# Two attention mixers and two hybrid blocks on one core: where a few small transposes stand between the projection products

## The reference, cut to what matters

```python
xbc = jax.nn.silu(causal_depthwise_conv(xbc, conv_w, conv_b))
xs, bm, cm = jnp.split(xbc, [SSM_INNER, SSM_INNER + SSM_GROUPS * D_STATE], axis=-1)
y = ssd_chunked(xs, dt, a_neg, bm, cm) + d_skip[:, None] * xs
y = rmsnorm_2(y * jax.nn.silu(z), ssm_norm)   # in two groups of 512
return jnp.concatenate([attn, y], axis=-1) @ w_out
```

## Time and profile before

| | |
|---|---|
| runs, median (lowest to highest) | 850.31 us (849.8 to 850.94) |
| the profiled execution: its time, and its span from first to last instruction | 850.76 us, 848.4 us |
| busy: PE, DVE, ACT, POOL | 841.2, 623.7, 535.3, 201.4 us |
| the chain that ended last, by engine | PE 94%, ACT 4%, DVE 1%, issue 1% |
| TensorE clock granted | 0.999 over the span |
| DMA | 146.19 MB, mean 172 GB/s |

### The profile page before, as it was taken

One profiled execution on the slowest core, in us unless ns is written; L12 is line 12 of the kernel. 1 busy time (PEld: TensorE's weight loads), 2 busy tenths in 40 slices (PEclk: granted clock), 3 DMA queues, 4 the chain that ended last, 5 costly groups with the idle time before them and its releaser, 6 DMA issues.

```text
span 848.4 us, 12997 instructions
## 1 busy us (share of the span) xinstructions
PE 841.2 (99%) x4631; PEld 706.4 (83%) x4631; DVE 623.7 (74%) x1109; ACT 535.3 (63%) x1035; POOL 201.4 (24%) x175
## 2 busy tenths in 40 slices
PE   9999999999999999999999999999999999999997
PEld 6887888888888888888888888888888888888885
DVE  6867865778776797688888546576797688888544
ACT  7677466866897864655556434787874655665533
POOL 0221053110152420033333000152330043334000
PEclk9999999999999999999999999999999999999999
DMA  9823563445534436665665555444347566565631
GB/s 319 297 72 132 165 205 128 150 149 182 172 125 148 140 133 200 205 201 182 186 196 190 207 199 176 151 149 149 103 147 224 176 200 196 186 180 184 228 116 49
DMA packets 94307, 146.19 MB, mean 172 GB/s; under 512 B 5925, under 2 KB 54565, under 8 KB 94245
## 3 DMA queue, kind: packets, MB, share of 16 engines
q1 hardware_dynamic: 92212, 139.58, 50.5%
q0 software_dynamic: 1296, 4.72, 1.6%
q10 hardware_dynamic: 736, 1.07, 0.4%
HBM read 144.32 MB, written 1.05 MB: 171 GB/s over the span
## 4 chain that ended last, share of the span: by engine, by line
PE 94%; ACT 4%; DVE 1%; issue 1%; POOL 0%; ACTq 0%; DVEq 0%
PE bank L1396 54%; PE bank L1349 17%; PE bank L1352 9%; PE bank L1273 6%; PE bank L1577 1%; PE bank L1481 1%; PE bank L1457 1%; ACT hi L1596 1%; PE bank L1454 1%; ACT hyb_prob L1812 1%; PE bank L1484 1%; PE bank L1278 0%; PE bank L1294 0%; PE bank L1292 0%; PE bank L1289 0%
## 5 line engine op out<-in xcount | busy, mean ns | idle before, releaser
L1182 DVE TENSOR_TENSOR lo<-raw,hi 128x1024 fp32r<-128x1024 f32 x242 | 308.7, 1293 | 106.8 <-ACT hi L1596 106.6
L1596 ACT ACTIVATE hi<-raw 128x1024 fp32r<-128x1024 f32 (+1 forms) x258 | 269.5, 1061 | 141.5 <-PE bank L1396 74.2
L1396 PE MATMUL bank<-hi,xT 128*128 128x512 f32 (+2 forms) x800 | 251.8, 386 | 0.0
L1396 PEld LDWEIGHTS bank<-hi,xT 128*128 128x128 f32 x800 | 147.3, 188 | 30.8 <-issue 4.3
L1396 PE MATMUL bank<-lo,xT 128*128 128x512 f32 (+2 forms) x400 | 151.2, 378 | 0.0
L1349 PE MATMUL bank<-xT,hi 128*128 128x512 f32 x640 | 149.5, 390 | 0.0
L1349 PEld LDWEIGHTS bank<-xT,hi 128*128 128x128 f32 x640 | 118.7, 188 | 24.3 <-DVE quarter L2192 0.6
L1396 PE MATMUL bank<-hi,hT 128*128 128x512 f32 x348 | 107.8, 390 | 0.0
L1396 PEld LDWEIGHTS bank<-lo,xT 128*128 128x128 f32 x400 | 75.4, 189 | 12.0
L1352 PE MATMUL bank<-xT,lo 128*128 128x256 f32 x640 | 80.6, 283 | 0.0
L1352 PEld LDWEIGHTS bank<-xT,lo 128*128 128x128 f32 x640 | 79.4, 192 | 1.4
(11 more groups left out here) (287 smaller groups left out, 1100.1 us busy)
## 6 DMA issues: line engine op xcount, KB each, us to landing
raw<-in_w_in SPq DMA_DIRECT2D x26, 1024.0 KB, 5.0
raw<-in_w_down SPq DMA_DIRECT2D x22, 1024.0 KB, 4.9
raw<-in_w_out SPq DMA_DIRECT2D x20, 1024.0 KB, 5.0
raw<-in_w_gate SPq DMA_DIRECT2D x20, 1024.0 KB, 5.3
raw<-in_w_up SPq DMA_DIRECT2D x20, 1024.0 KB, 5.3
raw<-in_w_in_b SPq DMA_DIRECT2D x10, 1024.0 KB, 5.1
raw<-in_w_in_a SPq DMA_DIRECT2D x7, 1024.0 KB, 7.7
raw<-in_w_in_a SPq DMA_DIRECT2D x8, 256.0 KB, 5.3
```

The source lines that it names most:

```text
L1182: return engine.tensor_tensor(lo[r][:, cols], raw[c.i % RAW][:, cols], hi[r][:, cols].bitcast(F32), ALU.subtract)
L1396: last = nc.tensor.matmul(bank[:, 0:wd], still[a], mv[r][:, off:off + wd], start=c.first and i == 0 and j == 0, stop=(c.last or c.closes a ...
L1596: nc.scalar.activation(hi[c.i % SPLIT][:, cols], raw[c.i % RAW][:, cols], ACT.Copy)\
```

## The change

In both mixers the first `turn_gate` of the second half moves from after the first chunk of the output product to between the two halves of that chunk, right behind `att(5)`, which holds the last two `pv4` steps. In both hybrids the first half of convolution piece 0 moves half a chunk later, to stand right ahead of the second half; the first half of piece 1 moves half a chunk later too, from behind `att(2)` to right ahead of its second half; and the second `turn_y` of group 1 moves half a chunk earlier, right behind the first. Nothing that is computed changes.

```diff
@@ mixer_ab
     out_product(sc, w_out, KD, {
-        0: (att(5), [lambda: turn_gates(sc, a, 1, 0)]),
+        0: (att(5) + [lambda: turn_gates(sc, a, 1, 0)], ()),
         1: ([lambda: turn_gates(sc, a, 1, 1)], ())}, mid)
@@ hybrid
     b = halves(sc, w_in, [(x0, 512)], do(norm_probs, sc, a, "scalar", 0, 4) + do(sums), att(1),
-               do(norm_probs, sc, a, "vector", 4, 2) + do(conv, 0, 0))
-    sc.goes_on(do(conv, 0, 1) + do(norm_probs, sc, a, "vector", 6, 2))
+               do(norm_probs, sc, a, "vector", 4, 2))
+    sc.goes_on(do(conv, 0, 0) + do(conv, 0, 1) + do(norm_probs, sc, a, "vector", 6, 2))
     evac_x(b, 1)
-    b = halves(sc, w_in, [(x0 + 512, 512)], do(conv_silu, 0), att(2) + do(conv, 1, 0), do(conv, 1, 1))
+    b = halves(sc, w_in, [(x0 + 512, 512)], do(conv_silu, 0), att(2), do(conv, 1, 0) + do(conv, 1, 1))
     evac_x(b, 2)
@@ hybrid, out_product
-        3: (do(turn_y, 1, 0), do(turn_y, 1, 1))})
+        3: (do(turn_y, 1), ())})
```

## The result

| | median | lowest to highest | span of the profiled execution |
|---|---|---|---|
| before, beside it on the same chip | 850.33 us | 849.7 to 850.94 | 848.4 us |
| after | 853.79 us | 853.43 to 854.78 | 852.0 us |

The ratio is 1.0043, with a 95% interval of 1.0033 to 1.0054: 3.46 us more, where +1.16 was predicted and 852.9 us was the high end of the range. The granted clock was 0.999, as before.

What follows compares the result with a forecast made beforehand. PE's own instructions, start to start, were taken to bound the kernel. Two waits +1.44, two ways back from pv4 -0.24 and four joinings -0.04 gave +1.16 on 850.31, so 851.5 us, range 850.0 to 852.9.

Steps and rivals of the forecast that it cites:

- what bounds the kernel: Whole kernel: PE's own instructions, start to start, set the time, and any new wait of PE is paid in full.
- the hybrids' piece 0: Both hybrids, `att(2)`: DVE divides heads 6 and 7 late, PE waits; 0.72 us each, 1.44 for both.
- the late-signal rival: Hybrids: ACT begins piece 0 only behind all eight transposes; waits 1.16 each, 852.3 us; chance 0.20, shared with other DVE lengthening.
- the one without a wait: Hybrids: scalings come in time all the same, only the joinings are left, -0.28, 850.0 us; chance 0.10.
- piece 1 and y: Hybrids: no PE wait, about 7 us and 1.7 us to spare; piece 1 gains nothing, y 0.01 us.
- the mixers' `split_o` and multiplication ahead of the low parts: Mixers, ACT and DVE: the `rest` step's split waits some 1.3 us longer, covered by some 8 us; cost nothing.
- the case without cover: Mixers: if the some 8 us of cover for the `rest` step's split were gone, cost 1.3 us; no chance given.
- my list of where else PE might wait: Signs of being wrong: PE waits at the gate for POOL, at y, or at a bank a late `conv` holds.
- the turn joined to pv4: Both mixers: the gate's four transposes right behind pv4 save PE a way back; 0.12 us each, 0.24 together.
- 0.6 us for a lone four: PE, four transposes alone: what the skill's 275 ns first transpose would make them need; the rows gave 0.45.
- The other joinings: Hybrids, piece 0 and y: two stretches of four transposes made one of eight; 0.01 us each, 0.04 for four.
- the rival of a full way back saved: All six joinings: each saves 0.21 us, 1.3 together; 850.4 us with the waits, 849.0 without; chance 0.03.

Runs made afterwards that it cites:

- e1: Kernel before plus only the mixers' move of the gate's turn to right behind `att(5)`: 852.78 us, ratio 1.0030.
- e2: Kernel before plus only the joining of convolution piece 0 in the hybrids: 851.73 us, ratio 1.0015.
- e3: Kernel before plus only the moves of convolution piece 1 and the turns of y: 849.99 us, ratio 0.9995.
- e4: Kernel before plus the mixers' move, with `att(5)` no longer holding low parts, so DVE makes held ones a step earlier: 850.14 us, ratio 0.9998.
- e5: Kernel before with only PE's four gate transposes moved behind pv4; DVE's multiplication and ACT's and DVE's `split_o` stay at the old place: 849.68 us, ratio 0.9998.
- e7: Kernel before plus the mixers' move, with the second mixer's three DVE casts made one chunk later: 851.99 us, ratio 1.0023.
- e8: Whole change against kernel before, with `att(5)` not holding low parts and heads 6 and 7 divided ahead of piece 0: 849.68 us, ratio 0.9996.
- e9: Kernel before without any joining, each mixer's four low parts at the first output chunk held one step longer: 864.64 us, ratio 1.0162.
- e6: Kernel before plus piece 0 joined in the hybrids, with heads 6 and 7 divided ahead of it on DVE: 850.01 us, ratio 1.0001.

## Why the prediction was wrong, by its steps

**Right: what bounds the kernel.** New waits of PE were paid in full. In the mixers 2 x (0.92 + 0.07) + 0.50 + 0.11 of refilling = 2.6, less the joinings, against 2.52 in e1.

**Right: the hybrids' piece 0.** Predicted 0.72 for each; from the start of the four turns to the start of the eight it is 259.46 - 258.28 = 1.18 us in the first hybrid and 580.26 - 579.15 = 1.11 in the second, where four turns take 0.44, so 0.74 and 0.67, with the named releaser; e2 alone gives 1.47. The signal comes with its own four transposes (1.56 after the start of eight), so the late-signal rival falls; so does the one without a wait.

**Right: piece 1 and y.** No wait, by e3 and by the changed kernel.

**Wrong: the mixers' `split_o` and multiplication ahead of the low parts.** The step that failed reads: "That split waits some 1.3 us longer ... but it is of the chunk that PE begins one and a half chunks later, some 8 us", and from there "Cost nothing". So the term put at nothing cost 2.5 us. The step rested on the place of `rest` in the list and on what is normally due there. What is due there in this stretch is more: two holds in a row had left four low parts, the first two for the chunk that PE begins next. So both numbers of the step were wrong. Before, the first low part was there at about 77.03 + 2.29 / 2 = 78.2 and PE's next chunk began at 84.13 (right behind the four transposes that then stood at 83.78): a cover of 5.9 us, not 8. After, it is there at 84.85, 6.7 us later and not 1.3, since DVE's wait for ACT's copy of pv4 (4.65 us) now stands ahead of it, with the multiplication and both parts of `split_o`. That the 1.3 us which I named for the case without cover comes near the 0.99 that each break cost is chance. That case had no chance of its own among the rivals: my list of where else PE might wait names POOL, y and a bank, not a low part. DVE's rows from 77 to 84 us, four `lo` ahead of the multiplication, stood in the trace of before, and I had them before me for both mixers; but the prediction goes by POOL's and PE's rows there and takes DVE's queue from the list. e4 and e5 show the cause: either edit puts the low parts ahead of the multiplication again, the one by making them earlier, the other by making it later, and the 2.52 us go.

**Wrong, but small: the third break.** The casts of the second mixer were not in the prediction; 0.6 us by the rows (0.50 and 0.11 of refilling), 0.36 by the medians of e7 and e1.

**Too large: the turn joined to pv4.** Predicted 0.12 for each. The rows of the first mixer give 0.10 for leaving pv4 (0.32 instead of 0.22), 81.26 - 80.85 = 0.41 for the four transposes and 0.09 for the way back (81.58 - 81.26 = 0.32): 0.60 against 0.66, a gain of 0.06. The four took 0.41 here and not 0.36. The prediction held 0.6 us for a lone four against its rows; the group's record is that long (0.60, each transpose's own some 0.27), but records overlap, and what PE pays is the 0.36 to the next start. The other joinings show 0.02 to 0.04 in the timelines, too little for e3, e5 or e8 to tell from nothing. So the rival of a full way back saved, 6 x 0.21 = 1.3, falls by the rows, and by e8 narrowly: with every wait taken out, e8 is 0.15 us below the kernel before, at most 1.1 by its interval.

**The sum as it was.** +1.41 (hybrids, predicted 1.44) + 2.5 (mixers, predicted -0.24) - some 0.1 = +3.8, measured +3.46 with an interval of 2.8 to 4.6. What lies between is within what the runs tell: the first hybrid's query turns stood at 223.1 us in the profile of before and at 222.6 in those of e2 and e3, which change nothing ahead of them.

## What to carry to other kernels

A step that is moved in an ordered list takes the whole of an in-order engine's queue with it: ask, for each engine of the step, what now stands behind it, and read that engine's rows of that stretch rather than what the list says is due there, since holds and deferrals may have heaped up the work of several steps. An operation that waits long (4.65 us for a copy) should not stand ahead of ready work that another engine wants soon; in e4 and e6 the same joining costs nothing once the ready work goes first. And price the case without cover as a rival with a chance, when the cover was worked out from a rule and not read from a row.

## What the runs showed of the hardware that was not expected

**A long break costs twice.** In e9 the rows show PE idle for 3.35 us in the first mixer and 6.14 in the second (3.59 and 6.38 lost from start to start), and the matmuls after it ran slower:

```profile
87.26 0.76 PE L1399 MATMUL bank<-hi,oT_hi 128*128 128x512 f32 x1 [3.35 <-issue]
87.82 0.63 PE L1399 MATMUL bank<-lo,oT_hi 128*128 128x512 f32 x1
88.25 0.63 PE L1399 MATMUL bank<-hi,oT_lo 128*128 128x512 f32 x1
...
92.52 0.87 PE L1276 MATMUL bank<-cst,quarter 128*128 128x128 f32 x4
93.14 0.47 PE L1399 MATMUL bank<-hi,oT_hi 128*128 128x512 f32 x1
```

The windows of that stretch (stretch, its length, busy us and count of PE, PE's weight loads, DVE, ACT and POOL, then the granted clock of PE, DMA share and GB/s):

```profile
80.00:83.00 3.00, 3.00 (x19) 2.34 (x16) 0.00 (x0) 1.64 (x3) 0.88 (x1) 1.00 0.00 0
87.30:92.50 5.20, 5.20 (x12) 3.95 (x13) 4.40 (x4) 0.00 (x0) 0.00 (x0) 0.50 0.53 187
93.50:96.00 2.50, 2.50 (x13) 2.03 (x12) 1.77 (x6) 1.59 (x2) 0.00 (x0) 1.00 0.78 297
```

Before the break the granted clock is 1.00 (2.4 GHz), behind it 0.50 (1.2 GHz), and twelve products go at 0.427 us from start to start instead of 0.23: 12 x 0.197 = 2.4 us. In the second mixer the clock is 0.50 behind the break too (197 to 200 us), again with twelve products at 0.427. Together that is the 4.8 us that e9's expectation lacks. With the four transposes behind each twelve (92.52 to 93.14 = 0.62 us, and 0.49 in the second, instead of 0.36) the slow stretches cost 2.7 and 2.5 us; with the 3.59 and 6.38 of the breaks that makes 15.2, and the profiled execution of e9, 865.10 us, stands 15.1 above the kernel before. The Trainium skill, "TensorE: Matmul & The Clock Gate", Part 1, has the array fall to 1.2 GHz when it has been idle; the rows agree. One of e9's four runs took 861.58 us and the others 864.18 to 865.63; its mean granted clock was 0.994 against 0.991 to 0.993. Whether the clock fell only once there is open, since that run left no trace. The breaks of 0.5 to 0.9 us in the changed kernel left the clock at 1.00.

**A wait without a releaser.** Four kernels (the changed one, e1, e7 and e9) show PE waiting for a DVE low part as "issue". The row could be read as a cost of PE itself; e4, which moves nothing but DVE's low parts, and e5, which leaves PE's joined stretch as it is, make it vanish. In all four breaks that these traces of the changed kernel and e9 show, PE goes on 0.17 us behind the end of the first low part, as worked out from DVE's rows (84.85, 186.23, 87.09 and 196.60 against 85.02, 186.40, 87.26 and 196.77). What a pause adds beyond itself is small: the first matmul behind it holds the next for 0.30 to 0.34 instead of 0.23.
